# Head of a transformer-block kernel: where x, the first weights and the modulation stand

## The chip, the cores and the metric

The kernel runs on one core of a Trainium2 chip. The metric is the device time of one execution in microseconds, as the median of several runs; the smaller the better. TensorE multiplies, VectorE and ScalarE work on SBUF and PSUM, GpSimd on SBUF, and SyncE issues most of the DMAs. Each engine works through its own list of instructions in order; semaphores join the lists.

## What is computed

Two transformer blocks on 1024 tokens of width 1024, all in float32. Only the head of the first block matters here: the modulation, the norm of x and the context, and the first projections.

```python
def adaln(cond, w_ada, b_ada):
    m = jax.nn.silu(cond) @ w_ada + b_ada
    return jnp.split(m, 3, axis=-1)
...
    shift, scale, gate = adaln(c, w_ada, b_ada)
    shift_c, scale_c, gate_c = adaln(c_ctx, w_ada, b_ada)
    h = rmsnorm(x, norm_g) * (1 + scale[:, None]) + shift[:, None]
    hc = rmsnorm(ctx, norm_g) * (1 + scale_c) + shift_c
    q, k, v, za, u, bg, cg, zc = jnp.split(h @ w_in, SPLIT_POINTS, axis=-1)
```

## The kernel before

Everything is feature-major: 1024 features are 8 groups k of 128 partitions, tokens lie along the free dimension. A float32 product is made of three fp32r matmuls, from high and low parts: `act_hi`, `act_lo` of the activations and `w_hi`, `w_lo` of the weights (`project`, L3015 to L3019; a weight tile of 128 output features takes 8 row sets, one for each k, of 6 matmuls of 512 columns). GpSimd makes the two parts of each weight tile (`split`, L743 CAST and L745 TENSOR_TENSOR) from `raw`.

The head runs as follows. SyncE's queue loads constants, then `w_ada` in four chunks of 2 MB (`ada_load`), x in three pieces (4, 2 and 2 groups; `x_in`, `kv_in`, `x_rest`), weight tiles 0 and 1, later the context and the rows of `w_gate`. Chunk n holds the columns of shift and scale for the groups 2n and 2n+1.

- The modulation: TensorE multiplies the condition vectors (`cond4`, 4 columns: two conditions and two of zeros) with a chunk, 8 plain fp32 matmuls of 512 columns (`ada_plain`, L3062), ScalarE copies the 4x512 result to `mrow` (`ada_row`, L1019), TensorE turns it to columns by four transposes (`turn_rows`, L3087), VectorE adds bias and multiplies by the norm's gain (`modulation`, L1960 to L1966), for four groups at a time: `modulation(0)` needs chunks 0 and 1, `modulation(1)` chunks 2 and 3. The second half of chunk 2 is multiplied from rounded parts: ScalarE (`ada_hi`, L1010) and VectorE (`ada_lo`, L1948) make them in the still free groups 4 and 5 of `act_hi` and `act_lo`, and `ada_parts` (L3074) multiplies them as 8 fp32r matmuls.
- The norm of x: ScalarE squares each group (L1024), VectorE adds the squares up (`accumulate`, L1876, L1879, into `acc0b`), TensorE sums over partitions (`sum_squares`, L3043, 8 one-column matmuls), ScalarE takes the root, VectorE the reciprocal (L1890), TensorE spreads it over the partitions (`spread`, L3053, 8 matmuls with the identity).
- The first rows: VectorE scales a group (`x_scaled`, L1975), ScalarE adds the shift and rounds to the high part (L991), VectorE makes the low part (`x_low`, L1981). `first_rows(s, ks)` multiplies tile s with the groups ks.

`clock_kept(n)` (L3081) is n matmuls of constants into an unused bank. The order on every engine is written out by hand. After the head come the attention pairs (from the first matmul of L2999), the rest of block one and block two. GpSimd's first split waits for `const_ready` 5, which VectorE gives with the last rounded part.

## Time and profile before

| | us |
|---|---|
| median of 3 runs | 2437.44 |
| lowest and highest run | 2437.38, 2437.7 |
| span of the profiled execution | 2433.8 |
| TensorE busy (98% of the span) | 2394.8 |
| VectorE busy (60%) | 1459.3 |
| GpSimd busy (40%) | 982.1 |
| ScalarE busy (39%) | 951.4 |
| 16 DMA engines, mean rate over the span | 112 GB/s |

The profile is of one execution, taken by the hardware profiler. Its span runs from the first to the last instruction, so it is somewhat shorter than the device time. The timeline gives each run of like instructions with its start and its length. A plain fp32 matmul appears as two rows of the timeline's count, an fp32r matmul as one. The ends of matmuls are modelled, so their starts are the better measure: the time of a group is read from its start to the next group's start. The granted clock is the share of 2.4 GHz that TensorE was given; 0.50 is the low level of 1.2 GHz.

### The profile page before, as it was taken

Reading aid. Unit: us, or ns where it says so; the run is one execution under the profiler, and the core shown is the slowest. Engines: PE = TensorE matmul, PEld = TensorE weight load, DVE = VectorE, ACT = ScalarE, POOL = GpSimd, SP = SyncE. Lnnn points to the kernel's source line nnn. Section 1 sums busy time; section 2 is a strip of 40 time slices with the busy share of each in tenths; the row PEclk is TensorE's granted clock in tenths of the full one; section 3 lists DMA queues with packets and bytes.
Section 4 is the critical chain, followed back from the end, with each engine's and each line's share of the span. In section 5 each row is a group of like instructions: output and inputs, shape, how many; then the busy total and the mean of one; then the engine's idle time right before and its main releaser. Section 6 shows DMA issues by size and latency. Waiting matters only on the chain. (4 is left out here: it accounts for less than half of the span.)

```text
span 2433.8 us, 33823 instructions
## 1 busy us (share of the span) xinstructions
PE 2394.8 (98%) x12088; PEld 1995.5 (82%) x12088; DVE 1459.3 (60%) x2340; ACT 951.4 (39%) x1759; POOL 982.1 (40%) x776
## 2 busy tenths in 40 slices
PE   9999999999999999999999999999999999999998
PEld 4888888887888888888888888887877888888886
DVE  5865656476464446446454653445576666798878
ACT  4443434344133444434434520234243333444443
POOL 1323132222482222222222232311357666699785
PEclk9999999999999999999999999999999999999999
DMA  8513131223453221222122244211314444644442
GB/s 308 175 35 124 36 106 60 87 72 114 148 191 96 83 60 59 70 84 74 52 74 78 83 139 172 96 52 44 95 48 152 160 160 147 233 161 159 147 148 86
DMA packets 87144, 271.92 MB, mean 112 GB/s; under 512 B 10056, under 2 KB 10184, under 8 KB 82000
## 3 DMA queue, kind: packets, MB, share of 16 engines
q1 hardware_dynamic: 64560, 184.37, 22.7%
q10 hardware_dynamic: 22432, 85.60, 10.9%
q8 instruction: 86, 1.41, 0.2%
q14 instruction: 66, 0.54, 0.1%
HBM read 198.08 MB, written 58.23 MB: 105 GB/s over the span
## 5 line engine op out<-in xcount | busy, mean ns | idle before, releaser
L743 POOL CAST w_hi<-raw 128x1024 fp32r<-128x1024 f32 x112 | 120.5, 1076 | 1079.2 <-issue 369.7
L2999 PE MATMUL ps<-act_hi,w_hi 128*128 128x512 f32 x1248 | 499.0, 400 | 1.9 <-DVE act_lo L2641 1.1
L3001 PE MATMUL ps<-act_hi,w_lo 128*128 128x512 f32 x1248 | 488.5, 391 | 0.0
L3000 PE MATMUL ps<-act_lo,w_hi 128*128 128x512 f32 x1248 | 486.7, 390 | 0.0
L745 POOL TENSOR_TENSOR w_lo<-raw,w_hi 128x1024 fp32r<-128x1024 f32 x112 | 278.0, 2482 | 9.0
L3001 PEld LDWEIGHTS ps<-act_hi,w_lo 128*128 128x128 f32 x1248 | 234.2, 188 | 52.0
L2999 PEld LDWEIGHTS ps<-act_hi,w_hi 128*128 128x128 f32 x1248 | 234.6, 188 | 45.1 <-DVE act_lo L2641 1.5
L3000 PEld LDWEIGHTS ps<-act_lo,w_hi 128*128 128x128 f32 x1248 | 234.9, 188 | 40.6
L3015 PE MATMUL ps<-act_hi,w_hi 128*128 128x512 f32 x384 | 150.2, 391 | 1.6 <-POOL w_lo L745 1.2
L3017 PE MATMUL ps<-act_lo,w_hi 128*128 128x512 f32 x384 | 149.6, 390 | 0.0
L3019 PE MATMUL ps<-act_hi,w_lo 128*128 128x512 f32 x384 | 118.3, 389 | 0.0
L3762 PE MATMUL ps<-act_hi,w_more 128*128 128x512 f32 x252 | 98.7, 392 | 2.2 <-DVE sq L2742 1.5
L2203 DVE TENSOR_TENSOR pt_lo<-ps,pt_hi 128x640 fp32r<-128x640 f32 (+1 forms) x64 | 50.5, 789 | 73.1 <-ACT pt_hi L1177 72.9
L2557 DVE TENSOR_TENSOR p_lo<-ps,p_hi 128x128 fp32r<-128x128 f32 (+3 forms) x64 | 48.5, 758 | 73.5 <-ACT p_hi L1510 73.5
L1177 ACT ACTIVATE pt_hi<-ps 128x640 fp32r<-128x640 f32 (+1 forms) x64 | 43.5, 680 | 122.5 <-PE ps L3252 122.5
L2808 DVE TENSOR_TENSOR w_more<-raw,w_more 128x256 fp32r<-128x256 f32 (+1 forms) x92 | 62.6, 680 | 44.4 <-ACT w_more L1698 44.4
L3764 PE MATMUL ps<-x_own,w_first 128*128 128x512 f32 x224 | 87.2, 389 | 0.0
L3015 PEld LDWEIGHTS ps<-act_hi,w_hi 128*128 128x128 f32 x384 | 72.1, 188 | 18.2 <-issue 2.5
L3019 PEld LDWEIGHTS ps<-act_hi,w_lo 128*128 128x128 f32 x384 | 72.1, 188 | 15.2
L3017 PEld LDWEIGHTS ps<-act_lo,w_hi 128*128 128x128 f32 x384 | 72.1, 188 | 15.0
L864 POOL TENSOR_TENSOR w_more<-w_more_f,w_more 128x256 fp32r<-128x256 f32 (+1 forms) x79 | 84.0, 1064 | 0.0
L3762 PE MATMUL ps<-x_own,w_first 128*128 128x512 f32 x192 | 74.9, 390 | 0.0
(548 smaller groups left out, 5843.0 us busy)
## 6 DMA issues: line engine op xcount, KB each, us to landing
raw<-in_w_stream_dram SPq DMA_DIRECT2D x192, 512.0 KB, 3.6
x_own_f<-a_dram SPq DMA_DIRECT2D x32, 512.0 KB, 5.7
a_dram<-stage SPq DMA_DIRECT2D x18, 512.0 KB, 6.2
ada<-in_w_ada_dram SPq DMA_DIRECT2D x4, 2048.0 KB, 21.5
spill<-res ACTq DMA_DIRECT2D x16, 512.0 KB, 4.9
gate_dram<-gate_sb ACTq DMA_DIRECT2D x32, 256.0 KB, 2.0
stage<-spill ACTq DMA_DIRECT2D x16, 512.0 KB, 4.1
act_lo_f<-a_dram SPq DMA_DIRECT2D x16, 512.0 KB, 5.4
```

Of the source, the lines that this page charges most:

```text
L743: nc.gpsimd.tensor_copy(w_hi[:, s, :, :], raw[:, s, :, :]).then_inc(S["w_hi"], 1)
L745: nc.gpsimd.tensor_tensor(w_lo[:, s, :, :], raw[:, s, :, :], w_hi[:, s, :, :].bitcast(F), ALU.subtract).then_inc(S["w_split"], 1)
L864: nc.gpsimd.tensor_tensor(w_slot(W_LO, n, i), whole, w_slot(W_HI, n, i).bitcast(F), ALU.subtract).then_inc(S["wv_lo"], 1)
L2808: nc.vector.tensor_tensor(w_slot(W_LO, n, i), whole, w_slot(W_HI, n, i).bitcast(F), ALU.subtract).then_inc(S["wv_late"], 1)
L2999: nc.tensor.matmul(out, wh, xh, start=start, stop=False, skip_group_check=onto)
L3000: nc.tensor.matmul(out, wh, xl, start=False, stop=False, skip_group_check=onto)
L3001: return nc.tensor.matmul(out, wl, xh, start=False, stop=stop, skip_group_check=onto)
L3015: nc.tensor.matmul(out, w_hi[:, s, k, :], part(xh, k, c, n), start=(first and k == ks[0]), stop=False)
L3017: nc.tensor.matmul(out, w_hi[:, s, k, :], part(xl, k, c, n), start=False, stop=False)
L3019: last = nc.tensor.matmul(ps[:, b0 * BANK + c:b0 * BANK + c + n], w_lo[:, s, k, :], part(xh, k, c, n), start=False, stop=(whole and k == k ...
L3762: nc.tensor.matmul(out, hi[:, w], x_hi(k), start=(not onto and k == 0), stop=False, skip_group_check=onto)
L3764: nc.tensor.matmul(out, hi[:, w], x_lo(k), start=False, stop=False, skip_group_check=onto)
```

## The change

- SyncE's queue: x's three pieces come first, then tile 0, chunk 0, tile 1, chunks 1, 2, 3. Tiles 2 and 3 are asked for ahead of the gate rows. The condition vector is written out by ScalarE's queue (`cond_kept`).
- TensorE: sum of squares and spread of x come ahead of all modulation; chunk 0, its turn and chunk 1 follow, then the row sets, with chunk 2 and chunk 3 between them. The spread is done by transposes. Chunk 2 is multiplied like the others; the rounded parts are gone on ScalarE, VectorE and TensorE.
- VectorE: `modulation(n)` does one chunk, two groups, in two instructions rather than four, ahead of each pair of scaled groups.
- ScalarE: all eight squares and the root ahead of the first `ada_row`.
- GpSimd: the first split waits only for its tile.

The diff, without its context and small declarations:

```diff
...
-        ADA_OUT = [0, 1, 4, 5]
+        ADA_OUT = [0, 1, 5, 5]
...
-        def turned_rows(i):
-
+        def turned_rows(n, m):
+
+            i = 8 * (m // 2) + 2 * n + m % 2
             return bank(4, 4 * i, 4 * i + 4)
...
-            ada_load(0)
             sp.dma_start(res[:, 0:4, :], x_t[:, 0:4, :]).then_inc(S["x_in"], 16)
-            ada_load(1)
             sp.dma_start(res[:, 4:6, :], x_t[:, 4:6, :]).then_inc(S["kv_in"], 16)
             sp.dma_start(res[:, 6:8, :], x_t[:, 6:8, :]).then_inc(S["x_rest"], 16)
+            tile_load(0)
+            ada_load(0)
+            tile_load(1)
+            ada_load(1)
             ada_load(2)
-            tile_load(0)
-            tile_load(1)
             ada_load(3)
             sp.wait_ge(S["ada_used"], 1)
             sp.dma_start(ctxT[:, :, :], ctx_r).then_inc(S["rows_in"], 16)
             sp.wait_ge(S["rows_in"], 16)
             sp.wait_ge(S["ada_used"], 2)
             sp.dma_start(ctxF[:, :, :], ctx_t).then_inc(S["rows_in"], 16)
-            sp.wait_ge(S["c_sig"], 2)
-            sp.dma_start(cond_dram.rearrange("k p -> p k"), cond4[:, :, 0], allow_slow_non_contiguous=True
-                         ).then_inc(S["ada_in1"], 16)
+            tile_load(2)
+            tile_load(3)
             sp.wait_ge(S["ada_used"], 3)
             for m in range(2, 6):
                 gate_load(m)
             sp.wait_ge(S["ada_used"], 4)
             for m in range(2):
                 gate_load(m)
-            tile_load(2)
-            tile_load(3)
...
-            pool.wait_ge(S["const_ready"], 5)
             split(0, 0, free=False)
             split(0, 1, free=False)
...
-            act.wait_ge(S["c_sig"], 2)
-            nc.scalar.activation(cond4r[:, :, 0:2], cond4[:, :, 0:2], ACT.Copy).then_inc(S["c_sig"], 1)
             act.wait_ge(S["const_ready"], 1)
             nc.scalar.activation(rsum[:, 0:1], eps[:, :], ACT.Sqrt)
-
-            def ada_hi():
-
-                act.wait_ge(S[ADA_IN[2]], 16)
-                for j in range(2):
-                    nc.scalar.activation(act_hi[:, 4 + j, :],
...
-            for k in range(4):
+            def cond_kept():
+
+                act.wait_ge(S["c_sig"], 2)
+                act.dma_start(cond_dram.rearrange("k p -> p k"), cond4[:, :, 0], allow_slow_non_contiguous=True
+                              ).then_inc(S["ada_in1"], 16)
+
+            for k in range(KT):
                 x0_square(k)
+            norm_rms("x0")
             ada_row(0)
-            for k in range(4, KT):
-                x0_square(k)
-            ada_row(1)
-            norm_rms("x0")
-            ada_hi()
...
-            norm_hi("x0", {2: [lambda: ada_row(2)],
-                           4: [lambda: ada_row(3), lambda: ctx_square(0), lambda: ctx_square(1), ctx_rms]})
+            norm_hi("x0", {2: [lambda: ada_row(1), cond_kept], 4: [lambda: ada_row(2)],
+                           6: [lambda: ada_row(3), lambda: ctx_square(0), lambda: ctx_square(1), ctx_rms]})
...
-            dve.wait_ge(S["c_sig"], 3)
-            nc.vector.tensor_tensor(cond4r[:, :, 2:4], cond4[:, :, 0:2], cond4r[:, :, 0:2].bitcast(F), ALU.subtract
-                                    ).then_inc(S["c_sig"], 1)
-
-            def ada_lo():
-
-                for j in range(2):
-                    dve.wait_ge(S["c_sig"], 5 + j)
-                    nc.vector.tensor_tensor(act_lo[:, 4 + j, :],
-                                            ADA_SLOT[2][:, 2 * j + 4:2 * j + 6, :].rearrange("p k c -> p (k c)"),
-                                            act_hi[:, 4 + j, :].bitcast(F), ALU.subtract).then_inc(S["const_ready"], 1)
-
-            def modulation(h):
-
-                k = slice(4 * h, 4 * h + 4)
...
                 both = mod[:, 0:16, :].rearrange("p (a k) c -> p a k c", a=2)[:, :, k, :]
-                rows = bank(4, 0, 32).rearrange("p (a k c) -> p a k c", a=2, c=4)
+                rows = bank(4, 0, 64).rearrange("p (a k c) -> p a k c", a=2, c=4)[:, :, k, 0:2]
                 bias = (vec[:, V_BADA:V_BADA + 16].rearrange("p (a k o) -> p a k o", a=2, o=1)[:, :, k, :]
-                        .to_broadcast([P, 2, 4, 2]))
-                dve.wait_ge(S["ada_turned"], 2 * h + 2)
-                nc.vector.tensor_copy(both, rows[:, :, :, 2:4]).then_inc(S["ada_step"], 1)
-                dve.wait_ge(S["ada_step"], 4 * h + 1)
-                nc.vector.tensor_tensor(both, rows[:, :, :, 0:2], both, ALU.add).then_inc(S["ada_step"], 1)
-                dve.wait_ge(S["ada_step"], 4 * h + 2)
-                nc.vector.tensor_tensor(both, both, bias, ALU.add).then_inc(S["ada_step"], 1)
-                dve.wait_ge(S["ada_step"], 4 * h + 3)
-                nc.vector.scalar_tensor_tensor(out=gs[:, k, :], in0=mod[:, 8 + 4 * h:12 + 4 * h, :], scalar=1.0,
+                        .to_broadcast([P, 2, 2, 2]))
+                dve.wait_ge(S["ada_turned"], n + 1)
+                nc.vector.tensor_tensor(both, rows, bias, ALU.add).then_inc(S["ada_step"], 1)
+                dve.wait_ge(S["ada_step"], 2 * n + 1)
+                nc.vector.scalar_tensor_tensor(out=gs[:, k, :], in0=mod[:, 8 + 2 * n:10 + 2 * n, :], scalar=1.0,
                                                in1=vec[:, V_NORM:V_NORM + 8].rearrange("p (m o) -> p m o", o=1)[:, k, :]
-                                               .to_broadcast([P, 4, 2]), op0=ALU.add, op1=ALU.mult
+                                               .to_broadcast([P, 2, 2]), op0=ALU.add, op1=ALU.mult
                                                ).then_inc(S["ada_step"], 1)
-                dve.wait_ge(S["ada_step"], 4 * h + 4)
+                dve.wait_ge(S["ada_step"], 2 * n + 2)
...
-            modulation(0)
             norm_rstd("x0")
-            ada_lo()
             dve.wait_ge(S["rstd_spread"], 1)
             for k in range(0, KT, 2):
-                if k == 4:
-                    modulation(1)
+                modulation(k // 2)
                 x_scaled(k)
                 x_scaled(k + 1)
+                if k == 6:
+                    norm_rstd("ctx")
                 x_low(k)
                 x_low(k + 1)
-                if k == 4:
-                    norm_rstd("ctx")
...
-                    last = nc.tensor.matmul(ps[:, b * BANK + t * P:b * BANK + (t + 1) * P],
-                                            rt[:, j:j + 1].to_broadcast([P, P]), ident, start=True, stop=True)
+                    last = nc.tensor.transpose(ps[:, b * BANK + t * P:b * BANK + (t + 1) * P],
+                                               rt[:, j:j + 1].to_broadcast([P, P]), ident)
...
+            def ada_plain(n):
 
                 pe.wait_ge(S[ADA_IN[n]], 16)
-                for k in range(rows):
-                    last = nc.tensor.matmul(ps[0:4, ADA_OUT[n] * BANK:(ADA_OUT[n] + 1) * BANK], cond4[:, k, :], ADA_SLOT[n][:, k, :],
-                                            start=(k == 0), stop=(k == KT - 1))
-                return last
-
-            def ada_parts():
-
-                out = ps[0:4, 4 * BANK:5 * BANK]
-                for j in range(2):
-                    pe.wait_ge(S["const_ready"], 4 + j)
-                    for k in range(2):
-                        x = slice(k * BANK, (k + 1) * BANK)
-                        for part in (act_hi, act_lo):
-                            last = nc.tensor.matmul(out, cond4r[:, 2 * j + 4 + k, :], part[:, 4 + j, x],
-                                                    start=False, stop=(j == 1 and k == 1 and part is act_lo))
+                for k in range(KT):
+                    last = nc.tensor.matmul(ps[0:4, ADA_OUT[n] * BANK:(ADA_OUT[n] + 1) * BANK], cond4[:, k, :],
+                                            ADA_SLOT[n][:, k, :], start=(k == 0), stop=(k == KT - 1))
                 last.then_inc(S["ada_used"], 1)
...
                 for _ in range(n):
-                    nc.tensor.matmul(bank(7), ident, con[:, 0:BANK], start=True, stop=True)
+                    nc.tensor.matmul(bank(3), ident, con[:, 0:BANK], start=True, stop=True)
 
             def turn_rows(n):
 
                 pe.wait_ge(S["ada_rows"], n + 1)
                 for m in range(4):
-                    last = nc.tensor.transpose(turned_rows(4 * (m // 2) + 2 * (n % 2) + m % 2),
-                                               mrow[:, n % 2, m * P:(m + 1) * P], ident[0:4, 0:4])
+                    last = nc.tensor.transpose(turned_rows(n, m), mrow[:, n % 2, m * P:(m + 1) * P], ident[0:4, 0:4])
                 last.then_inc(S["ada_turned"], 1)
 
             pe.wait_ge(S["small_in"], 48)
             clock_kept(4)
-            pe.wait_ge(S["c_sig"], 4)
-            ada_plain(0, KT).then_inc(S["ada_used"], 1)
+            sum_squares("x0")
+            spread("x0")
+            clock_kept(1)
+            pe.wait_ge(S["c_sig"], 2)
+            ada_plain(0)
+            clock_kept(1)
+            turn_rows(0)
             clock_kept(3)
-            ada_plain(1, KT).then_inc(S["ada_used"], 1)
-            turn_rows(0)
-            clock_kept(1)
-            sum_squares("x0")
-            turn_rows(1)
-            spread("x0")
-            ada_plain(2, 4)
-            ada_parts()
-            ada_plain(3, KT).then_inc(S["ada_used"], 1)
-
-            tile_ready(T_ATT)
-            tile_ready(T_ATT + 1)
+            ada_plain(1)
...
-            for k in range(4):
-                first_rows(0, [k])
-                first_rows(1, [k])
-                if k == 0:
-                    turn_rows(2)
-                    turn_rows(3)
+            tile_ready(T_ATT)
+            first_rows(0, [0])
+            turn_rows(1)
+            tile_ready(T_ATT + 1)
+            first_rows(1, [0])
+            first_rows(0, [1])
+            first_rows(1, [1])
+            ada_plain(2)
+            first_rows(0, [2])
+            turn_rows(2)
+            first_rows(1, [2])
+            ada_plain(3)
+            first_rows(0, [3])
+            turn_rows(3)
+            first_rows(1, [3])
             first_rows(0, range(4, 6))
             pe.wait_ge(S["ada_step"], 8)
             spread("ctx")
...
```

Two places in the order of instructions. On TensorE, from the program's start to the first row set, before (`ps<-con` 128x512 are the constants' matmuls, `con,acc0b` the sum of squares, `con,rt` the spread, `con,mrow` the turns):

```order
L3081 MATMUL ps<-con 128x512 x4
L3062 MATMUL ps<-ada,cond 4x512 x8
L3081 MATMUL ps<-con 128x512 x3
L3062 MATMUL ps<-ada,cond 4x512 x8
L3087 MATMUL ps<-con,mrow 128x4 x4
L3081 MATMUL ps<-con 128x512
L3043 MATMUL ps<-con,acc0b 128x1 x8
L3087 MATMUL ps<-con,mrow 128x4 x4
L3053 MATMUL ps<-con,rt 128x128 x8
L3062 MATMUL ps<-ada,cond 4x512 x4
```

and with the change, up to the first two matmuls of the first row set:

```order
L3039 MATMUL ps<-con 128x512 x4
L3013 MATMUL ps<-con,acc0b 128x1 x8
L3023 MATMUL ps<-con,rt 128x128 x8
L3039 MATMUL ps<-con 128x512
L3032 MATMUL ps<-ada,cond 4x512 x8
L3039 MATMUL ps<-con 128x512
L3045 MATMUL ps<-con,mrow 128x4 x4
L3039 MATMUL ps<-con 128x512 x3
L3032 MATMUL ps<-ada,cond 4x512 x8
L2985 MATMUL ps<-act_hi,w_hi 128x512
L2987 MATMUL ps<-act_lo,w_hi 128x512
```

Two chunks stood ahead of the sum of squares; now none does, and two stand between the spread and the rows. Further on TensorE's list, the row sets of group 2 and what now stands ahead of and between them:

```order
L3032 MATMUL ps<-ada,cond 4x512 x8
L2985 MATMUL ps<-act_hi,w_hi 128x512
L2987 MATMUL ps<-act_lo,w_hi 128x512
L2985 MATMUL ps<-act_hi,w_hi 128x512
L2987 MATMUL ps<-act_lo,w_hi 128x512
L2989 MATMUL ps<-act_hi,w_lo 128x512 x2
L3045 MATMUL ps<-con,mrow 128x4 x4
```

Before, the row sets of groups 1 to 5 followed each other with nothing between; chunk 3 comes in the same way ahead of group 3.

## Rows read from the trace of the kernel before

**Rows 1.** The page's head: span of the profiled execution.

```profile
span 2433.8 us, 33823 instructions
```

**Rows 2.** Windows, core 0: span, busy us of each engine, granted clock, DMA share, GB/s.

```profile
73.20:2424.50 2351.30, 2327.47 (x11861) 1960.60 (x11860) 1416.13 (x2290) 917.78 (x1715) 967.54 (x764) 1.00 0.32 105
```

**Rows 3.** Timeline of TensorE, head: start us, us, operation, [idle before].

```profile
4.11 6.77 PE L3081 MATMUL ps<-con 128*128 128x512 f32 x8 [4.11 <-DMA cond<-in_cond_t_dram]
11.14 7.03 PE L3062 MATMUL ps<-ada,cond 128*4 128x512 f32 x16 [0.27 <-DMA ada<-in_w_ada_dram]
18.10 2.84 PE L3081 MATMUL ps<-con 128*128 128x512 f32 x6
20.87 7.03 PE L3062 MATMUL ps<-ada,cond 128*4 128x512 f32 x16
27.83 0.41 PE L3087 MATMUL ps<-con,mrow 4*128 4x4 f32 x4
...
29.66 2.56 PE L3043 MATMUL ps<-con,acc0b 128*128 128x1 f32 x16 [0.36 <-DVEq L1987]
...
33.85 3.78 PE L3053 MATMUL ps<-con,rt 128*128 128x128 f32 x16 [1.12 <-DVE rt L1890]
37.56 3.61 PE L3062 MATMUL ps<-ada,cond 128*4 128x512 f32 x8
...
43.05 7.03 PE L3062 MATMUL ps<-ada,cond 128*4 128x512 f32 x16
50.01 0.50 PE L3015 MATMUL ps<-act_hi,w_hi 128*128 128x512 f32 x1
...
73.24 0.39 PE L2999 MATMUL ps<-act_hi,w_hi 128*128 128x512 f32 x1
```

**Rows 4.** Timeline of ScalarE, squares of x.

```profile
15.89 3.90 ACT L1024 ACTIVATE act_lo_f<-res 128x1024 f32<-128x1024 f32 x4 [9.62 <-DMA res<-in_x_t_dram]
...
25.77 2.00 ACT L1024 ACTIVATE act_lo_f<-res 128x1024 f32<-128x1024 f32 x2 [0.47 <-DMA res<-in_x_t_dram]
```

**Rows 5.** Timeline of VectorE, head.

```profile
16.98 0.69 DVE L1876 COPY acc0b<-act_lo_f 128x1024 f32<-128x1024 f32 x1 [12.02 <-ACT act_lo_f L1024]
17.93 3.88 DVE L1879 TENSOR_TENSOR acc0b<-acc0b,act_lo_f 128x1024 f32<-128x1024 f32 x3 [0.25 <-ACT act_lo_f L1024]
24.39 5.21 DVE L1879 TENSOR_TENSOR acc0b<-acc0b,act_lo_f 128x1024 f32<-128x1024 f32 x4 [2.58 <-ACT act_lo_f L1024]
...
40.17 4.90 DVE L1981 SCALAR_TENSOR_TENSOR act_lo<-stage,mod,act_hi 128x1024 fp32r<-128x1024 f32 x2
...
47.48 2.48 DVE L1981 SCALAR_TENSOR_TENSOR act_lo<-stage,mod,act_hi 128x1024 fp32r<-128x1024 f32 x2
...
54.28 0.17 DVE L1966 SCALAR_TENSOR_TENSOR gs<-mod,vec 128x8 f32<-128x8 f32 x1
```

**Rows 6.** Timeline of GpSimd, second weight split.

```profile
39.63 1.05 POOL L743 CAST w_hi<-raw 128x1024 fp32r<-128x1024 f32 x1
40.76 3.23 POOL L745 TENSOR_TENSOR w_lo<-raw,w_hi 128x1024 fp32r<-128x1024 f32 x1
```

**Rows 7.** Windows of 1 us; PEclk is the granted clock.

```profile
31.00:32.00 1.00, 1.00 (x6) 1.00 (x6) 0.00 (x0) 0.00 (x0) 0.00 (x0) 0.50 1.06 438
...
38.00:39.00 1.00, 1.00 (x4) 0.26 (x3) 1.00 (x2) 0.01 (x1) 1.00 (x1) 1.00 0.61 238
```

**Rows 8.** Timeline of TensorE, narrow matmuls and transposes at full clock.

```profile
78.68 1.84 PE L3147 MATMUL ps<-con,res 128*128 128x2 f32 x16
...
85.00 1.07 PE L3155 MATMUL ps<-con,res 128*128 128x128 f32 x8
```

**Rows 9.** DMA issues to 160 us, and VectorE's first gate sum.

```profile
res<-in_w_gate_dram SPq DMA_DIRECT2D x2, 512.0 KB, 11.8
...
74.38 1.28 DVE L2023 CUSTOM_DVE_ANT_0 gate_w<-gate_w,res,vec 128x1024 f32<-128x1024 f32 x1
```

**Rows 10.** Waits of TensorE from 60 us: total us, times, longest.

```profile
PE ps L3719 <- DVE mp L2660: 4.1, 8, 1.2
```

6 lines of the change are left out of this document (2 added, 4 removed).

## Prediction

> **What bounds the kernel now.** I read the windows first: from 73.2 us to 2424.5 us TensorE is busy 2327.5 of 2351.3 us at the full granted clock [rows 2]. What moves its start into that stretch moves the end of the program, unless some of the 23.8 us of holes closes. Those holes are waits of TensorE for VectorE, ScalarE or GpSimd, whose work there hangs on TensorE's own results; a later start shifts both sides. So the question is when the first tiles' rows are done, now at 73.24 (the first matmul of L2999) [rows 3]. The program itself is 2437.44 us, 3.6 more than the profiled span of 2433.8 [rows 1]; I carry a shift of the span over to the median one to one.
>
> The timeline of TensorE then tells what fills the head [rows 3]. The modulation product of one chunk, 8 fp32 matmuls that the trace shows as 16 rows, takes 6.96 us (43.05 to 50.01). Two of them run at 11.14 and 20.87, while x is still loading and being squared: ScalarE squares x from 15.89 to 27.8 [rows 4], VectorE adds the squares up to 29.6 [rows 5]. Only then come sum of squares (29.66), spread of the reciprocal roots (33.85), the third chunk (37.56 to 43.05), the fourth, and the rows from 50.01 on. In short: half of the modulation now lies in the shadow of x's chain, and behind 29.66 TensorE is all but gapless. The reader is to see that the wait for x costs nothing while something else fills it.
>
> **The change, part by part.**
>
> *x ahead of the modulation weights.* The first 2 MB had landed by 11.1, when the first chunk's product began [rows 3]; in the same place x's first half will. From 15.89 to 25.77, 4 MB landed (a chunk and x's other half) [rows 4]: 2.47 us a MB. That puts x's second half at 16.0, weight tile 0 at 17.3, chunk 0 at 22.2, tile 1 at 23.5, chunks 1 to 3 at 28.4, 33.4, 38.3. ScalarE needs 3.9 us for four squares, so all eight are done by 19. VectorE's copy begins 1.1 us after the landing, its first addition 2.0 after (16.98 and 17.93 against 15.89), and additions follow at 1.33 us ((5.21 - 1.23)/3) [rows 5]: 13.15 + 6 x 1.33 + 1.23 = 22.35 instead of 29.6.
>
> *Weight split in the middle of it.* GpSimd no longer waits for the rounded parts, so it splits tile 0 at 17.3, beside the additions. The one place where its split ran beside VectorE work with two SBUF operands: CAST and TENSOR_TENSOR at 39.63 and 40.76 [rows 6], and two low parts took 4.90 us there against 2.48 alone [rows 5]. The price is 2.4, and 0.3 more for the CAST of tile 1 at 23.5 (a CAST alone, by the first 0.5 us of that overlap): x's sums are ready at 25.0. Bounds: 0 if they pass each other (22.35), and a second 2.1 if tile 1's TENSOR_TENSOR gets in ahead of the last addition (27.1).
> The Trainium skill (SBUF — State Buffer, Who interferes with whom) has VectorE with two SBUF inputs and a reading GpSimd instruction exclude each other for the whole instruction. By that the split would cost VectorE up to its whole 4.3 us (1.05 + 3.23), and the end would move by up to 1.9 us more. The 4.90 us speak for a smaller price than the rule's.
>
> *TensorE idle and at the low clock.* Nothing fills TensorE from 10.9 to 25. In the trace the granted clock goes to the low level (0.50, 1.2 GHz) at 31, in the middle of one-column matmuls, and is full again at 38, after the spread [rows 7]. At the program's start the first four wide matmuls took 6.77 us for 8 rows, against 2.84 us for 6 rows later [rows 3]: 0.85 and 0.43 us a row. After 14 us of rest I take the low level for sum, spread and the wide matmul behind. The sum: 16 narrow rows took 1.84 us at the full clock [rows 8], so about 3.5. The spread is by transposes now: 8 rows, 1.07 at full clock [rows 8], 2.1 at low, instead of 3.78. The gap between sum and spread was 1.6 us, of which VectorE's modulation steps held the reciprocal for 0.8: 0.85. One wide matmul: 1.7. End: 25.0 + 3.5 + 0.85 + 2.1 + 1.7 = 33.15. Bounds: all at full clock, 3.6 less; the low level lasting 6.8 us from the spread on, as at the start, 1.5 more on the first chunk.
>
> *What stands ahead of the rows.* Chunk 0 (landed long since) 6.96, one wide matmul 0.86, its four turned rows 0.34 (ScalarE's copy lies under the wide matmul), three wide ones 2.6, chunk 1 6.96: 17.7, so the rows begin at 50.9 instead of 50.01. VectorE needs 0.4 for the two steps of a chunk (0.17 each and their waits), 2.5 for two scalings (taken as two low parts, 2.48) and 1.3 for a low part [rows 5] from 41.2 on: ready at 45.5, no wait.
>
> *What now stands between the rows.* Before, 50.01 to 73.24 held the 16 row sets, two turns and the context's spread: 23.23. To these come chunks 2 and 3, whole, 13.92; one more turn, 0.34; less 0.1 as the context's spread is transposes. End of the head: 50.87 + 13.92 + 23.23 + 0.24 = 88.3, against 73.24: **+15.0 us**. The dropped fp32r parts (chunk 2 took 5.49 us with them, 37.56 to 43.05, and 6.96 without) cost 1.5 of that; it was the cheaper form. Their VectorE and ScalarE work lay under the spread and gives TensorE nothing.
>
> *Under cover.* The last pair's chain is the closest: its turn ends at 75.7, VectorE has scaled both by 78.6 and put out the sixth low part at 79.9, TensorE asks at 80.0. The context's part then ends about 1 us later against TensorE than before; before, TensorE first works on other things from 73.24 to the 16 narrow rows at 78.68 [rows 3, 8], and only then on the context, so it is covered; were it not, the 1 us would be added. The condition vector goes out from ScalarE's queue between two pairs' high parts instead of SyncE's: what stands behind it there is the high part of a pair that VectorE has not scaled yet, and on SyncE's queue the tiles 2 and 3 move ahead of the gate rows, which nobody misses. The gate rows are asked for when chunk 3 is used, at 74, the last at about 76; they landed 11.8 us after issue [rows 9], so at 88, and VectorE's gate sums stand at 74.38 + 15.0 = 89.4 [rows 9]. Cover of 1 us; were it gone, VectorE would be late by what is lacking, with 2 to 3 us of its own before TensorE waits.
>
> **The rivals.**
>
> *Smaller loss: no collision and a full clock.* GpSimd and VectorE pass each other (-2.6) and TensorE is granted the full clock at once (-3.6): 15.0 - 6.2 = +8.8, 2446.2. Against it: the 4.90 us, and the slow first 6.77 us of the program, which was itself behind a rest.
>
> *Larger loss: collisions twice, clock low into the chunk, gates late.* +2.1, +1.5 and about 1: 15.0 + 4.6 = 19.6, 2457.0. For it: tile 1 lands at 23.5, within 1 us of the last addition's start.
>
> *Faster: the later start is paid back behind the head.* The mechanism is the holes of TensorE behind 73.2: where TensorE waits for weights or for VectorE's side work (gate sums, splits) that would by then be done, a late TensorE finds it ready. It would decide if more than 15.0 of the 23.8 us of holes [rows 2] were waits for things that do not hang on TensorE. Against it: the loads there run at 105 GB/s [rows 2], a quarter of the head's 405 (1 MB in 2.47 us), and the waits view puts the holes down to VectorE's work on TensorE's results, the longest group 4.1 us in eight waits [rows 10]. If all holes closed: 2437.4 + 15.0 - 23.8 = 2428.6.
>
> *The change does not do what it says*, so that the rows start before the modulation is complete but TensorE's list is as short as before: the order of instructions excludes it, all 32 fp32 matmuls are there, behind the sum.
>
> **How the numbers follow.** TensorE's work behind x's sums is what decides: even from the earliest sums, 22.35, with everything at full clock, it ends at 88.3 - 6.2 = 82.1, later than 73.24. Forecast as reckoned, within 3 us of +15.0: 0.72. Smaller loss, +8.8 to +12: 0.11. Larger, +18 to +20: 0.14. Paid back: 0.02 faster. No visible change: 0.01. The predicted time is 2437.4 + 15.0 = 2452.4; the range takes in both bounds, 2446 to 2457.5. With 0.2% (4.9 us, about what a measurement of this kernel can tell from no change): slower 0.97, within 0.01, faster 0.02.
>
> **What would show it.** In the changed profile: x's first square at 11, the last addition ending near 25 with one or two additions of 2.5 to 3.4 us beside GpSimd's TENSOR_TENSOR; TensorE idle from 10.9 to 25; sum and spread at the low granted clock; the first row set at 51; two runs of 16 modulation rows between the row sets at about 57 and 67; the first L2999-like matmul of the next stage at 88; from there on a trace that is the old one moved. Wrong would be: the first chunk's product in the hole before 25, rows starting before 45, VectorE late for a row set, or a hole near the gate sums.

## The result and the profile after

The changed kernel takes 2457.05 us, the median of 4 runs (2456.08 to 2459.82); the kernel before took 2437.57 us beside it (4 runs, 2437.38 to 2438.27). The ratio is 1.0082, with a 95% interval of 1.0069 to 1.0094: slower by 19.5 us by the medians, by 20.0 us by the ratio. The forecast was slower by 15.0 us, 2452.4, with a range up to 2457.5. The direction and the mechanism were right. The size was not: the sum was 4.5 us too small, and the loss reaches the range's end.

The profiled run took 2457.65 us, with this span and these busy times:

```profile
span 2455.8 us, 33783 instructions
PE 2398.5 (98%) x12070; PEld 1994.9 (81%) x12070; DVE 1471.2 (60%) x2337; ACT 949.8 (39%) x1756; POOL 983.3 (40%) x776
```

The timeline of TensorE in the head is the counterpart of [rows 3] (start us, us, operation, [idle before <- what ended it]). L3039 are the matmuls with constants, L3013 the sum of squares, L3023 the spread, L3032 a chunk of the modulation, L3045 its turned rows, L2985 opens a row set:

```profile
4.09 5.96 PE L3039 MATMUL ps<-con 128*128 128x512 f32 x8 [4.09 <-DMA cond<-in_cond_t_dram]
26.23 3.57 PE L3013 MATMUL ps<-con,acc0b 128*128 128x1 f32 x16 [16.17 <-DVEq L1960]
30.39 1.97 PE L3023 MATMUL ps<-con,rt 128*128 128x128 f32 x8 [0.59 <-DVE rt L1878]
32.15 1.91 PE L3039 MATMUL ps<-con 128*128 128x512 f32 x2
34.00 8.00 PE L3032 MATMUL ps<-ada,cond 128*4 128x512 f32 x16
41.93 1.12 PE L3039 MATMUL ps<-con 128*128 128x512 f32 x2
42.99 0.41 PE L3045 MATMUL ps<-con,mrow 4*128 4x4 f32 x4
...
46.10 7.03 PE L3032 MATMUL ps<-ada,cond 128*4 128x512 f32 x16
53.06 0.50 PE L2985 MATMUL ps<-act_hi,w_hi 128*128 128x512 f32 x1
...
59.28 7.03 PE L3032 MATMUL ps<-ada,cond 128*4 128x512 f32 x16
...
69.76 7.03 PE L3032 MATMUL ps<-ada,cond 128*4 128x512 f32 x16
```

TensorE stands still for 16.17 us, where before the products of two chunks filled that place. All four chunks now lie behind the sum of squares, two of them between the row sets, at 59.28 and 69.76. The first matmul of the next stage, 73.24 before, comes at 91.28: the head is **18.0 us longer**, not 15.0.

VectorE's seven additions, the last three of them one by one, and GpSimd's first two weight splits in the same stretch:

```profile
13.54 12.63 DVE L1867 TENSOR_TENSOR acc0b<-acc0b,act_lo_f 128x1024 f32<-128x1024 f32 x7 [0.25 <-ACT act_lo_f L1010]
18.86 1.87 DVE L1867 TENSOR_TENSOR acc0b<-acc0b,act_lo_f 128x1024 f32<-128x1024 f32 x1
20.83 3.17 DVE L1867 TENSOR_TENSOR acc0b<-acc0b,act_lo_f 128x1024 f32<-128x1024 f32 x1
24.11 2.06 DVE L1867 TENSOR_TENSOR acc0b<-acc0b,act_lo_f 128x1024 f32<-128x1024 f32 x1
...
17.86 1.79 POOL L740 CAST w_hi<-raw 128x1024 fp32r<-128x1024 f32 x1 [17.40 <-DMA raw<-in_w_stream_dram]
19.73 3.20 POOL L742 TENSOR_TENSOR w_lo<-raw,w_hi 128x1024 fp32r<-128x1024 f32 x1
24.06 1.04 POOL L740 CAST w_hi<-raw 128x1024 fp32r<-128x1024 f32 x1 [1.13 <-DMA raw<-in_w_stream_dram]
```

The seven additions take 12.63 us from first to last. The first four take 1.22 to 1.23 us each, the last three 1.87, 3.17 and 2.06. Windows of 1 us (TensorE's busy time and count first; the third number from the end is the granted clock) give the clock:

```profile
35.00:36.00 1.00, 1.00 (x3) 0.13 (x1) 0.00 (x0) 0.00 (x0) 0.00 (x0) 0.50 0.81 344
36.00:37.00 1.00, 1.00 (x3) 0.17 (x2) 0.00 (x0) 0.00 (x0) 0.00 (x0) 1.00 0.31 131
```

It is at the low level (0.50, 1.2 GHz) already before the sum, and comes back to full only at 36, two microseconds into chunk 0, which therefore takes 8.00 us and not 7.03.

The span grew by 22.0 us, the head by 18.0. The other 4.0 us lie far behind the head. I matched the start of each of GpSimd's CASTs in the two traces. Up to 662 us of the kernel before, each is later by the head's 18.0, within 0.15 us. Across the stage that makes the memory's keys and values (662 to 740 us there) the difference grows by 3.3 us, and then it stays within 0.2 until 1771. The waits of TensorE (total us, times, longest) name the place; first the kernel after, then the same wait in the kernel before:

```profile
PE ps L2969 <- DVE mkv_out L2308: 4.8, 2, 4.0
```

```profile
PE ps L2999 <- DVE mkv_out L2338: 1.6, 2, 0.9
```

Whether the change causes these 4 us was the first question for the experiments; what fills the extra 3 us of the head was the second.

### The profile page after: what moved, and what is told of

It reads as the page before. It is cut to its first block and busy times, and to the rows that moved or that the text cites. A ratio compares the mean times of both kernels' runs of the same rounds, so it can differ in the third digit from the quotient of the medians.

```text
span 2455.8 us, 33783 instructions
## 1 busy us (share of the span) xinstructions
PE 2398.5 (98%) x12070; PEld 1994.9 (81%) x12070; DVE 1471.2 (60%) x2337; ACT 949.8 (39%) x1756; POOL 983.3 (40%) x776
## 3 DMA queue, kind: packets, MB, share of 16 engines
q8 instruction: 86, 1.41, 0.2%
## 5 line engine op out<-in xcount | busy, mean ns | idle before, releaser
L2985 PE MATMUL ps<-act_hi,w_hi 128*128 128x512 f32 x384 | 150.7, 392 | 1.6 <-POOL w_lo L742 1.2
L2985 PEld LDWEIGHTS ps<-act_hi,w_hi 128*128 128x128 f32 x384 | 72.1, 188 | 19.8 <-issue 4.2
L2987 PEld LDWEIGHTS ps<-act_lo,w_hi 128*128 128x128 f32 x384 | 72.1, 188 | 14.7
L860 POOL TENSOR_TENSOR w_more<-w_more_f,w_more 128x256 fp32r<-128x256 f32 (+1 forms) x79 | 78.7, 996 | 0.0
```

The source lines that it names most:

```text
L860: nc.gpsimd.tensor_tensor(w_slot(W_LO, n, i), whole, w_slot(W_HI, n, i).bitcast(F), ALU.subtract).then_inc(S["wv_lo"], 1)
L2985: nc.tensor.matmul(out, w_hi[:, s, k, :], part(xh, k, c, n), start=(first and k == ks[0]), stop=False)
L2987: nc.tensor.matmul(out, w_hi[:, s, k, :], part(xl, k, c, n), start=False, stop=False)
```

## The experiments

Each kernel was timed beside the kernel before on the same chip. That kernel's median was 2436.3 us beside the first four (7 runs), 2437.65 beside the next four (27 runs) and 2437.5 beside the last four (21 runs). "Head" is the start of the next stage's first matmul (73.24 before, 91.28 after). "Rest" is the span's change less the head's, against the first profile of the kernel before; for the changed kernel it is +3.96. Head and rest come from one profiled execution of each kernel, the time from the median of all its runs.

### The splits behind the additions

```diff
+            pool.wait_ge(S["acc_done"], 8)
             split(0, 0, free=False)
             split(0, 1, free=False)
```

> The changed kernel, but GpSimd's first split waits until the squares of x are added up (acc_done 8). Theory A (GpSimd's split of tile 0 beside the additions costs VectorE the whole of its CAST and TENSOR_TENSOR, 3.4 us, since seven additions took 12.63 us against 9.2 at 1.33 us each): the last addition ends at 22.8 instead of 26.2, the head ends 3.4 us sooner (88 instead of 91.3 us), the time falls from 2457 to about 2453.5. Rival B (the additions are slowed by the loads, not by GpSimd): no change in the additions and none in the time.

Measured: 2452.5 us, ratio 1.0064 (1.0047 to 1.0081); head 86.43.

```profile
12.62 9.20 DVE L1868 TENSOR_TENSOR acc0b<-acc0b,act_lo_f 128x1024 f32<-128x1024 f32 x7 [0.25 <-ACT act_lo_f L1011]
...
21.88 3.57 PE L3014 MATMUL ps<-con,acc0b 128*128 128x1 f32 x16 [11.03 <-DVEq L1961]
...
29.65 7.48 PE L3033 MATMUL ps<-ada,cond 128*4 128x512 f32 x16
```

The seven additions now take 9.20 us instead of 12.63, each 1.23. So VectorE lost 3.43 us to GpSimd, where I took 2.4 + 0.3. The three long additions of the changed kernel tell where: 0.64 beside the CAST of tile 0 (1.87 against 1.23), 1.94 beside its TENSOR_TENSOR (3.17), and 0.83 beside the CAST of tile 1 (2.06), which started at 24.06, 0.05 us ahead of the last addition. Alone, GpSimd's CAST takes 1.04 us here and its TENSOR_TENSOR 2.34. The head is 4.85 us shorter: 3.4 by this, 0.9 because x landed earlier in this run (the first addition starts at 12.62, not 13.54), and 0.5 because chunk 0 saw less of the low clock. The splits, now from 22.0 to 28.9, are late for nobody: the row sets begin at 48.19.

### Wide matmuls in the hole

```diff
-            clock_kept(4)
+            clock_kept(21)
             sum_squares("x0")
```

> The changed kernel with 17 more wide matmuls of constants in TensorE's hole (10.6 to 25.2 us). Theory A (the low granted clock comes from the hole and costs 1.75 in the sum, 0.8 in the spread, 1.0 in the wide matmul and 1.0 in the first chunk): full clock throughout, head 4.5 us shorter, 2452.5. Rival B (the one-column matmuls of the sum bring the clock down by themselves, as in the kernel before, where it fell 1.3 us into them): the sum is faster for its first part only, spread and wide matmul stay slow, head 1 to 2 us shorter, 2455 to 2456.

Measured: 2454.1 us, ratio 1.0075 (1.0058 to 1.0092); head 87.82.

```profile
4.20 20.40 PE L3039 MATMUL ps<-con 128*128 128x512 f32 x42 [4.20 <-DMA cond<-in_cond_t_dram]
25.44 1.95 PE L3013 MATMUL ps<-con,acc0b 128*128 128x1 f32 x16 [0.84 <-DVEq L1960]
27.98 1.09 PE L3023 MATMUL ps<-con,rt 128*128 128x128 f32 x8 [0.60 <-DVE rt L1878]
28.90 1.86 PE L3039 MATMUL ps<-con 128*128 128x512 f32 x2
30.69 7.84 PE L3032 MATMUL ps<-ada,cond 128*4 128x512 f32 x16
```

With TensorE kept at work, sum and spread run at the full level: 1.95 and 1.09 us instead of 3.57 and 1.97, as reckoned. But behind the 8 one-column matmuls (16 rows) and the spread the clock falls all the same, so the head comes out between the two theories. The wide matmul (1.86 for two rows, against 1.12) and the start of chunk 0 (7.84) are at the low level. So the rest of 16 us costs the sum and the spread 2.5 us; the low clock in chunk 0 came in this run also without it. The head is 3.45 us shorter, 0.8 of that by an earlier landing.

### One chunk in the hole

```diff
-            tile_load(0)
             ada_load(0)
+            tile_load(0)
...
             clock_kept(4)
-            sum_squares("x0")
-            spread("x0")
-            clock_kept(1)
             pe.wait_ge(S["c_sig"], 2)
             ada_plain(0)
-            clock_kept(1)
+            sum_squares("x0")
+            spread("x0")
```

> The changed kernel with chunk 0 loaded straight behind x and multiplied ahead of the sum of squares; the two wide matmuls around it are gone. Theory A (what costs is the list of TensorE behind x's sums, since the hole is empty): chunk 0 runs from 21.7 to about 30.4 (its first part at the low clock), the sum ends at 32.2, the spread at 34.7, rows begin at 45 instead of 53.1, the time is about 8 us less, 2449. Rival B (the rows wait for VectorE and ScalarE, whose chain is no shorter): rows begin as late as in the changed kernel, the same time.

Measured: 2450.2 us, ratio 1.0052 (1.0036 to 1.0069); head 84.57, 6.7 us less than the changed kernel.

```profile
21.30 9.90 PE L3032 MATMUL ps<-ada,cond 128*4 128x512 f32 x16 [10.56 <-DMA ada<-in_w_ada_dram]
31.14 1.95 PE L3013 MATMUL ps<-con,acc0b 128*128 128x1 f32 x16
```

The chunk lands at 21.3 behind x and takes 9.90 us, since most of it runs at the low clock. The sum of squares has to wait for it and comes five microseconds later than in the changed kernel. The additions took 9.20 us here, as GpSimd's split waits for a tile that lands behind the chunk. The head is shorter even so, and the time near theory A's 2449. What counts is how much of TensorE's work is left when x's sums are there.

### The kernel before, only later

```diff
+            for _ in range(20):
+                nc.tensor.matmul(bank(3), ident, con[:, 0:BANK], start=True, stop=True)
             tile_ready(T_ATT)
             tile_ready(T_ATT + 1)
```

> The kernel before with 20 wide matmuls of constants (17.2 us at the full clock) right ahead of the first row set, nothing else changed. Theory A (a later start is carried to the end one to one, and what the changed kernel loses behind 73 us comes from its other order of loads): +17.2 us, 2454.7. Rival B (any such delay shifts GpSimd's splits against VectorE's work near 700 us, where TensorE waited 4.0 us more in the changed kernel's profile): +18 to +21 us and a spread of the runs of some us, as the changed kernel has (2456.1 to 2459.8).

Measured: 2454.0 us, ratio 1.0071 (1.0054 to 1.0087); head 90.59, 17.35 later than before; the median rose by 17.7 us. A pure delay of the head comes back in the time almost one to one, so nothing behind it pays it back. In this profile the rest is +3.15:

```profile
PE ps L2999 <- DVE mkv_out L2338: 3.4, 2, 2.5
```

The same wait has grown, in a kernel with no part of the change.

### The kernel before, once more

The same code, timed as another kernel, 10 runs.

> The kernel before, unchanged, profiled once more, for the stretch from 662 to 740 us (the memory keys and values, where GpSimd splits weight tiles back to back). All five later kernels ran level with the kernel before up to 662 us behind the head, then lost 0.8 to 3.9 us to it there. Theory A (that stretch has a price that varies from run to run whatever the head does, and the profile of before was a cheap one): this profile shows a stretch 1 to 3 us longer than the first one, span 2435 to 2437. Rival B (only a delayed program pays it): the stretch is as in the first profile, within 0.3 us.

Measured: 2437.3 us, ratio 0.9997 (0.9988 to 1.0007); head 73.34; rest +2.0.

```profile
PE ps L2999 <- DVE mkv_out L2338: 2.7, 2, 1.8
PE ps L3762 <- DVE sq L2742: 2.5, 1, 2.5
```

Unchanged code has the longer waits as well, at both places where the traces differ. So the stage behind the head varies from run to run, and the profile on which the prediction rests was a cheap one. Its span was 3.6 us under the median, while the other profiled runs had a span 1.8 to 2.1 us under their own time.

### The kernel before with the short spread

```diff
-                    last = nc.tensor.matmul(ps[:, b * BANK + t * P:b * BANK + (t + 1) * P],
-                                            rt[:, j:j + 1].to_broadcast([P, P]), ident, start=True, stop=True)
+                    last = nc.tensor.transpose(ps[:, b * BANK + t * P:b * BANK + (t + 1) * P],
+                                               rt[:, j:j + 1].to_broadcast([P, P]), ident)
```

> The kernel before, but the reciprocal roots are spread by transposes, as in the changed kernel. Theory A (8 rows in place of 16 at the low clock): the spread takes 1.9 us instead of 3.8, the head ends 1.9 us sooner (71.3), the time falls by 1.5 to 2 us. Rival B (VectorE or the weights' split are as late as TensorE there): the chunk behind starts sooner but the rows begin at 50.0 as before, no gain.

Measured: 2437.95 us, ratio 0.9997 (0.9988 to 1.0006), 11 runs; head 70.94, 2.3 less.

```profile
32.91 1.62 PE L3053 MATMUL ps<-con,rt 128*128 128x128 f32 x8 [1.13 <-DVE rt L1890]
```

The spread takes 1.62 us where the fp32 matmuls took 3.78. The head moved as theory A has it, the time did not. The one part of the change that helps is worth 2.2 us of the head, but in the time it can't be told from nothing: in its profile the rest was +5.7, the wait for `mkv_out` 4.5 us.

### The changed kernel with the loads of before

```diff
+            ada_load(0)
             sp.dma_start(res[:, 0:4, :], x_t[:, 0:4, :]).then_inc(S["x_in"], 16)
+            ada_load(1)
...
+            ada_load(2)
             tile_load(0)
-            ada_load(0)
             tile_load(1)
-            ada_load(1)
-            ada_load(2)
...
             clock_kept(4)
-            sum_squares("x0")
-            spread("x0")
-            clock_kept(1)
             pe.wait_ge(S["c_sig"], 2)
             ada_plain(0)
-            clock_kept(1)
-            turn_rows(0)
             clock_kept(3)
             ada_plain(1)
+            turn_rows(0)
+            clock_kept(1)
+            sum_squares("x0")
+            turn_rows(1)
+            spread("x0")
+            ada_plain(2)
```

Chunk 3 stays between the row sets, the rounded parts stay away, and ScalarE puts out the rows of chunks 0 and 1 around its squares.

> The changed kernel with the loads of x and the chunks in the order of before, and chunks 0 and 1 multiplied ahead of the sum of squares, chunk 2 behind the spread, chunk 3 between the rows; the rest (chunk by chunk steps, no rounded parts, spread by transposes, chunk 3 among the rows) stays changed. Theory A (the whole loss is in the loads' order and in the chunks that stand behind x's sums): head ends at 73.4, within 1 us of before, time within 1.5 us of before. Rival B (the chunk by chunk steps and the whole chunk 2 have a price of their own): head 3 us or more longer than before.

Measured: 2437.7 us, ratio 1.0001 (0.9991 to 1.001), 10 runs; head 71.86, 1.4 less than before.

```profile
29.22 1.95 PE L3016 MATMUL ps<-con,acc0b 128*128 128x1 f32 x16 [0.34 <-DVEq L1963]
...
33.01 8.45 PE L3035 MATMUL ps<-ada,cond 128*4 128x512 f32 x16
```

The whole loss is gone, with modulation steps one chunk at a time, no rounded parts and a chunk between the row sets still in place. What costs is the order of the loads and the chunks behind x's sums. The collision is gone with it: tile 0 lands behind chunk 2 here, and its split starts at 31.69, when the additions are done.

### Both cures together

The wait of the first experiment, and `clock_kept(18)` in place of `clock_kept(4)`:

> The changed kernel with both edits: GpSimd's first split behind x's sums, and 14 more wide matmuls of constants in TensorE's hole. Theory A (collision and low clock are separate and add: 4.8 and 3.5 us of the head in the two runs alone): the head ends at 83, the time is 8 us under the changed kernel's, 2449. Rival B (they overlap): head at 86, 2452.

Measured: 2451.3 us, ratio 1.0054 (1.0039 to 1.0069); head 84.30.

```profile
21.89 1.95 PE L3014 MATMUL ps<-con,acc0b 128*128 128x1 f32 x16 [0.37 <-DVEq L1961]
24.43 1.97 PE L3024 MATMUL ps<-con,rt 128*128 128x128 f32 x8 [0.60 <-DVE rt L1879]
```

The head lies between the two theories' 83 and 86. Seven of the 18 us can be had back inside the changed order, with earlier sums and the full clock for the sum of squares and for chunk 0 (7.03 us); the spread is still at the low level. Of the seven, 0.9 are an earlier landing. The other 11 stay, with chunks 0 and 1 (14 us) behind the sum.

### The stage behind the head, in both kernels

In kv_split of the kernel before, and the same edit in the changed kernel. It leaves out the low parts of two weight tiles of the memory stage for seven of their eight rows groups:

```diff
-                nc.gpsimd.tensor_tensor(lo, raw[:, t % 2, :, :], hi.bitcast(F), ALU.subtract).then_inc(S["w_split"], 1)
+                n = 1 if j in (5, 6) else KT
+                nc.gpsimd.tensor_tensor(lo[:, 0:n], raw[:, t % 2, 0:n, :], hi[:, 0:n].bitcast(F), ALU.subtract
+                                        ).then_inc(S["w_split"], 1)
```

> The kernel before, with the low parts of two weight tiles of the memory stage (the sixth and seventh of its 16) made for an eighth of their rows only; the rest of those low parts is left out. GpSimd has 4 us less to do between 662 and 740 us. Theory A (what varies from run to run there is GpSimd's back-to-back splits, pushed by late weight loads and by VectorE): the stretch is at or under the level of the first profile, the median falls by 1 to 2.5 us and the range of the runs narrows from 5 us. Rival B (the variation comes from the loads alone, or from elsewhere): median within 0.5 us, range as wide.

> The changed kernel with the same two low parts left out for seven eighths of their rows. Theory A (the part of the loss behind the head is that stage's variation): the head stays at 91.3 and the rest falls to that of the first profile of before, span 2451.5 to 2452.5, median 2453.5. Rival B (it is spread over the program): median 2456 to 2457.

Measured, the kernel before: 2436.4 us, ratio 0.9993 (0.9984 to 1.0002), 11 runs; head 73.78; rest +0.16, the wait for `mkv_out` 1.6 us again. Measured, the changed kernel: 2453.7 us, ratio 1.0066 (1.005 to 1.0081); head 87.94; rest +0.9 instead of +3.96, and this stage's part of it 0.0 instead of 3.3. What remains of the rest lies at the second place (`sq`, 2.5 us). So where GpSimd has slack in this stage, both kernels go through it at the price of the first profile. One profile each is a thin base, and in the kernel before the median moved by 1.0 us only, which the interval doesn't settle.

The changed kernel's median came out as theory A has it, 2453.7 against 2453.5, but not for its reason: the head, which this edit does not touch, did not stay at 91.3. It is 3.3 us shorter, and below the forecast's 88.3. Its additions, the last of them, and the CAST of tile 1:

```profile
12.33 11.79 DVE L1869 TENSOR_TENSOR acc0b<-acc0b,act_lo_f 128x1024 f32<-128x1024 f32 x7 [0.25 <-ACT act_lo_f L1012]
22.90 1.23 DVE L1869 TENSOR_TENSOR acc0b<-acc0b,act_lo_f 128x1024 f32<-128x1024 f32 x1
...
22.90 2.12 POOL L740 CAST w_hi<-raw 128x1024 fp32r<-128x1024 f32 x1 [1.18 <-DMA raw<-in_w_stream_dram]
```

x landed 1.2 us earlier (first square at 10.30, not 11.51). Tile 1's CAST and the last addition started together, and this time the addition kept its 1.23 us, which saves 0.8. The clock was back by the start of chunk 0 (31.63), which took 7.03 us; with the wide matmul ahead of it that saves 1.3. So one and the same head code gave +18.0 in one profiled run and +14.7 in another; the latter was the fastest of its kernel's four runs, 2.5 us under their median.

### A head shorter than before's

The short spread, and on VectorE the reciprocal ahead of the four modulation steps:

```diff
-            modulation(0)
             norm_rstd("x0")
+            modulation(0)
...
             spread("x0")
+            pe.wait_ge(S["ada_step"], 2)
             ada_plain(2, 4)
```

> The kernel before with the spread by transposes and VectorE's reciprocal ahead of its modulation steps. Theory A: the sum's end to the spread's start falls from 1.5 to 0.6 us and the spread from 3.7 to 1.6, the head ends 3.1 us sooner (70.1), and the median falls by 3 us, if the rest is carried over one to one. Rival B (as with the transposes alone, where the head was 2.3 us shorter and the median 0.3 us longer: the rest takes it back): median within 1 us of before.

Measured: 2434.85 us (2431.7 to 2440.3, 11 runs), ratio 0.9994 (0.9985 to 1.0003); head 68.09, 5.15 less than before, about 0.8 of it by an earlier landing.

```profile
31.41 1.09 PE L3053 MATMUL ps<-con,rt 128*128 128x128 f32 x8 [0.26 <-DVE rt L1890]
32.43 3.60 PE L3062 MATMUL ps<-ada,cond 128*4 128x512 f32 x8
```

It has the shortest head and the lowest median of all, but its interval still holds 1. The profiled run is the fastest of the 11, 3.2 us under their median. The clock did not fall behind x's sums here: spread (1.09 against 1.62 in the kernel with the short spread alone) and half a chunk (3.60 against 4.71) are at the full level. That is worth 1.6 us, beside the 0.9 of idle time ahead of the spread that the edit closes.

### The loads alone

The kernel before, with the order of loads of the changed kernel and nothing else:

```diff
-            ada_load(0)
             sp.dma_start(res[:, 0:4, :], x_t[:, 0:4, :]).then_inc(S["x_in"], 16)
-            ada_load(1)
...
-            ada_load(2)
             tile_load(0)
+            ada_load(0)
             tile_load(1)
+            ada_load(1)
+            ada_load(2)
             ada_load(3)
```

> The kernel before with the loads alone in the changed kernel's order (x, tile 0, chunk 0, tile 1, chunks 1 to 3); TensorE's order is that of before, both chunks ahead of the sum. Theory A (TensorE works through its list as it lands; chunk 0 at 22, chunk 1 at 33, the sum at 41, the spread until 46, chunks 2 and 3, rows from 59): head ends at 82 to 83, 9 to 10 us later than before and 8 us sooner than the changed kernel. Rival B (moving the loads alone is as bad or worse than the change, since x's sums wait in vain): head at 91 or later.

Measured: 2450.7 us, ratio 1.0051 (1.0036 to 1.0066); head 86.83, 13.6 later than before.

```profile
22.41 9.93 PE L3062 MATMUL ps<-ada,cond 128*4 128x512 f32 x16 [12.75 <-DMA ada<-in_w_ada_dram]
...
43.30 1.84 PE L3043 MATMUL ps<-con,acc0b 128*128 128x1 f32 x16
```

The loads alone cost 13.6 of the 18.0 us; the head lies between the two theories. I can't put the other 4.4 down to the new order on TensorE. GpSimd's split still waits for the rounded parts in this kernel, so nothing slows the additions. With the splits behind the additions the changed kernel's head is 86.43 (x there 0.6 earlier), much the same as the 86.83 here. The old order has chunks 0 and 1 ahead of the sum, which then starts at 43.30; the new one has the sum early and the chunks behind it. Under these loads both end at about the same time.

All runs in one table (us; time change against the median of the kernel before on the same chip):

| kernel | head against 73.24 | rest of the span | change of the time |
|---|---|---|---|
| after | +18.0 | +4.0 | +19.5 |
| after, splits behind the additions | +13.2 | +3.9 | +16.2 |
| after, wide matmuls in the hole | +14.6 | +2.5 | +17.8 |
| after, one chunk in the hole | +11.3 | +6.6 | +13.9 |
| after, both cures | +11.1 | +4.7 | +13.6 |
| after, loads of before | -1.4 | +2.9 | 0.0 |
| after, splits relieved | +14.7 | +0.9 | +16.2 |
| before, only later | +17.35 | +3.15 | +17.7 |
| before, once more | +0.1 | +2.0 | -0.3 |
| before, short spread | -2.3 | +5.7 | +0.3 |
| before, splits relieved | +0.5 | +0.2 | -1.0 |
| before, shorter head | -5.15 | +1.25 | -2.6 |
| before, loads of after | +13.6 | +1.4 | +13.25 |

The last column is the head's, plus 1.4 to 3.2 us for the seven kernels built on after, and minus 1.5 to plus 0.4 for four of the six built on before. The two of these with a shorter head (-2.3, -5.15) gained 2.6 us less in time than at the head. These differences set a single run's head against a median. The profiled run lay 2.5 us under its kernel's median with the splits relieved in after and 3.2 with the shorter head, and 3.3 above it with one chunk in the hole.

## Why the prediction was right or wrong

In short: the path was right, and four terms were too small. The splits beside the additions cost 3.4 us and not 2.7, the low clock reached into chunk 0 (1.0, taken as 0), the pieces between the row sets and the wide matmuls cost 1.2 more than their own length, and the stretch behind the head, taken as a pure shift, gave the rest of the miss in the median (1.5, cause open).

**Right: what decides.** TensorE is full from x's sums on, and the chunks that used to lie in front of them now lie behind. With before's loads and its two chunks ahead of the sum the loss is 0 (71.86 head), and with a pure delay of 17.35 us it is 17.7. The hole from 10 to 26 us was there (16.17 us), the rows began behind two chunks, chunks 2 and 3 stood between the row sets at 7.03 us each, and no rival of the fast side showed: behind the head nothing was paid back.

**Right: the covers.** The last pair, the context's part and the gate rows kept their places; VectorE's gate sum started at 93.25, and no wait for it shows.

**Wrong: the price of the splits beside the additions.** This term was 2.4 + 0.3 us and measured 3.4 (12.63 against 9.20): 2.6 for tile 0's split and 0.8 for tile 1's CAST. The 2.4 came from two low parts that took 4.90 us instead of 2.48 [rows 5, 6]. One by one they are

```profile
40.17 1.58 DVE L1981 SCALAR_TENSOR_TENSOR act_lo<-stage,mod,act_hi 128x1024 fp32r<-128x1024 f32 x1
...
41.68 3.40 DVE L1981 SCALAR_TENSOR_TENSOR act_lo<-stage,mod,act_hi 128x1024 fp32r<-128x1024 f32 x1
```

that is 0.3 lost beside a CAST that had been running for 0.54 us, and 2.1 beside a TENSOR_TENSOR. I carried over the 0.3 as the price of a CAST. But what VectorE loses is what is left of GpSimd's instruction when VectorE's own comes up, and the CAST of tile 1 had just started: 0.8. Whether it gets in at all hung on hundredths of a microsecond (0.05 of lead here); in the changed kernel with the splits relieved it did not, and the additions lost 2.6 us. The Trainium skill (SBUF — State Buffer, Who interferes with whom) has the two engines exclude each other for the whole instruction. The trace agrees: the addition issued at 20.83 stood until the TENSOR_TENSOR (19.73 + 3.20 = 22.93) was as good as done and ended at 24.00. So the step that failed here is also the claim that the 4.90 "speak for a smaller price than the rule's"; that row agrees with the rule within 0.2 us. The 4.3 us that I worked out for it were too many because GpSimd's own wait is in the 3.23 of [rows 6]: alone it takes 2.34 to 2.36.

**Wrong: the low clock ends with the first wide matmul.** I took 0 for chunk 0, with 1.5 as a bound. It cost 1.0 (8.00 against 7.03). In the other runs it cost 1.4 in the old load order (8.45), 0.8 even when TensorE had not rested (7.84), 0.5 with the splits behind the additions (7.48), and nothing with both cures and with the splits relieved (7.03). So the term is not fixed by the program: it lay between 0 and 1.0 in the five profiles of the changed order that have chunk 0 behind the spread. The sum and the spread themselves were well sized: 3.57 and 1.97 against 3.5 and 2.1.

**The head's sum, stretch by stretch.** It lacks 3.0 us: x's sums are used at 26.23, not 25.0 (+1.2: 0.7 for the splits, 0.4 because x landed at 11.5 and not 11.1). From there to chunk 0 it took 7.77 us, not 8.15 (-0.4). From chunk 0 to the first row set 19.06, not 17.7 (+1.4: 1.0 by the clock, 0.4 in the four wide matmuls between). From the first row set to the head's end 38.2, not 37.4 (+0.8). I had costed a chunk and a turn between the row sets at their own length; each interruption also makes the last two matmuls ahead of it and the first behind it slower by 0.1 each (behind it, a recorded 0.50 us against 0.39), and there are four or five more of them. Only this last term and the 0.4 of the wide matmuls are the same in both profiles of this head code: the kernel with the splits relieved has them too (18.09 and 38.22 us for the two stretches). The 1.2 and the 1.0 are not there, x's sums are used at 24.18, and its head of 87.94 lies just under the forecast's 88.3. So of the 3.0 us some 1.2 are in the program; the other 1.8 are this run's, and in the other run they were -1.5.

**Wrong: the profiled span as the measure.** The rule "a shift of the span goes to the median one to one" held up to 662 us. The sentence "whose work there hangs on TensorE's own results" did not hold throughout: in the memory's key and value stage VectorE is late because of GpSimd, and GpSimd's start there hangs on loads (1.41 us of wait for one ahead of the CAST at 697.58). The first profile had this stage cheap. Of the 22.0 us between the two spans, some 2 are this. The medians differ by 19.5: 18.0 of the head and 1.5 that I put down to the stage, without a run that shows it as a mean. The forecast had this stretch at nothing; what it adds to the median stays open.

**A slip without effect.** The head's loads run at 424 GB/s (1 MB of 1,048,576 bytes in 2.47 us), not 405.

So the range was used up to its very end, since its bounds were taken one by one, each at its nearest row, and none for the stage behind the head. The larger rival's 19.6 came, but that is in good part luck. Of its three reasons the collision cost 0.7 more and not 2.1 (no second TENSOR_TENSOR got in), the low clock in the chunk 1.0 and not 1.5, and the gates were not late. The other 2.8 us it does not name: 1.3 in the head (the later landing, the wide matmuls, the interruptions between the row sets) and 1.5 behind it.

## What the runs leave open

Whether what lies behind the head costs more in the kernels built on after isn't settled. In their profiled runs TensorE waited 3.6 to 4.8 us for `mkv_out` (2.9 with the splits relieved), in those built on before 1.6 to 4.5. The two ranges overlap, and so do the rests in the table. Nor is it known how often the changed kernel's head is 91.3 and how often 87.9. The traces show how one run loses time in the stage of the memory's keys and values. VectorE (low part of a row group, L1894 after, L1906 before) and GpSimd (split) meet at almost the same moment. VectorE's row group is the same in both; GpSimd's weight tile is an earlier one after than before. GpSimd after:

```profile
698.71 2.40 POOL L788 TENSOR_TENSOR w<-raw,w 128x1024 fp32r<-128x1024 f32 x1
```

VectorE after:

```profile
698.73 3.46 DVE L1894 TENSOR_TENSOR act_lo<-stage,act_hi 128x1024 fp32r<-128x1024 f32 x1
...
703.42 3.18 DVE L1894 TENSOR_TENSOR act_lo<-stage,act_hi 128x1024 fp32r<-128x1024 f32 x1
```

and TensorE behind it:

```profile
707.35 0.36 PE L2969 MATMUL ps<-m_hi,w 128*128 128x256 f32 x1 [3.96 <-DVE mkv_out L2308]
```

Before, VectorE and GpSimd:

```profile
681.97 1.23 DVE L1906 TENSOR_TENSOR act_lo<-stage,act_hi 128x1024 fp32r<-128x1024 f32 x1
...
684.43 2.12 DVE L1906 TENSOR_TENSOR act_lo<-stage,act_hi 128x1024 fp32r<-128x1024 f32 x1
```

```profile
682.04 3.42 POOL L792 TENSOR_TENSOR w<-raw,w 128x1024 fp32r<-128x1024 f32 x1
```

Whoever starts first runs at its own length, and the other stands still meanwhile. Before, VectorE was first by 0.07 us: 1.23 us for it, 3.42 for GpSimd. After, GpSimd was first by 0.02 us: 2.40 for it, 3.46 for VectorE. `mkv_out` is queued behind on VectorE, and TensorE waits for it, 3.96 us. So a tile of weights that lands some tenths later can decide who is first; no run here moves one tile alone. Whether the changed load order makes the dear outcome likelier would need many traces of each kernel.

## What to carry to other kernels

A load can only be moved forward at the price of what it overtakes, and what decides is which work can fill TensorE while the chain behind the other load runs. Two chunks of 7 us in the shadow of x's sums were worth more than sums 3.4 us earlier. Where VectorE adds SBUF operands in a chain that TensorE waits for, count for any GpSimd CAST or TENSOR_TENSOR on SBUF that can start in it up to its whole length, or make it wait. A CAST of 1.04 us cost 0.3 to 0.8 here, a TENSOR_TENSOR of 2.34 us 1.9 to 2.1. And take a second profile of the kernel before where a few microseconds matter: two of unchanged code differed by 2.1 us of span, at two places. The same holds for the kernel after: two profiles of its head code differed by 3.3 us.
